# Attention scores of a hybrid encoder layer: 128-row matmuls over stacked high and low parts instead of pairs of 64-row matmuls, and a reordered prologue of three weight tiles

## The reference, cut to what matters

```
proj = h @ w_in[l]
qa, ka, va, qb, kb, vb, ga, gb = jnp.split(proj, pts, axis=-1)
...
# diff_attention: 8 heads, two 64-wide maps m = 0, 1 of each, chunk-causal, 128-query blocks
s = jnp.einsum('bqhmd,bkhmd->bhmqk', qb, k).astype(jnp.float32) * scale + bias[None, :, None]
s = jnp.where(mask, s, NEG_INF)
p = jax.nn.softmax(s, axis=-1)
attn = p[:, :, 0] - lam * p[:, :, 1]
return jnp.einsum('bhqk,bkhe->bqhe', attn, vf)
```

## Time and profile before

| | |
|---|---|
| median of the runs | 1826.25 us (3 runs, lowest 1825.3, highest 3576.29) |
| the profiled execution, its own time | 1823.93 us |
| its span from the first to the last instruction | 1822.1 us |
| granted TensorE clock, mean | 0.998 |
| busy share: PE, DVE, ACT, POOL | 98%, 58%, 39%, 36% |

### The profile page before, as it was taken

The page is one execution under the profiler, slowest core; times in us unless marked ns, Lnnn a source line. Parts: engine busy times, 40 slices in busy tenths (PEclk is TensorE's granted clock), DMA queues, the critical chain, the costliest instruction groups (busy, mean ns, idle before and its releaser), DMA issues.

```text
span 1822.1 us, 25660 instructions
## 1 busy us (share of the span) xinstructions
PE 1783.3 (98%) x9007; PEld 1453.0 (80%) x9007; DVE 1048.4 (58%) x2291; ACT 701.6 (39%) x1544; POOL 661.9 (36%) x662
## 2 busy tenths in 40 slices
PE   5999999999999999999999999999999999999998
PEld 4777777777778888888888878788888888888886
DVE  5366666656665554111432565677766666777767
ACT  5355555555556666310222132322223333222232
POOL 4311112111123444322222250465555656655560
PEclk9999999999999999999999999999999999999999
DMA  6411111111111101134322440121121111111112
GB/s 239 140 35 33 49 36 36 47 34 35 44 34 43 33 24 36 46 81 160 103 83 91 140 153 0 59 69 46 46 69 46 46 46 46 56 59 46 60 45 92
DMA packets 143398, 117.91 MB, mean 65 GB/s; under 512 B 23556, under 2 KB 130252, under 8 KB 143308
## 3 DMA queue, kind: packets, MB, share of 16 engines
q1 hardware_dynamic: 134092, 112.52, 20.1%
q10 hardware_dynamic: 9216, 4.20, 0.8%
HBM read 99.88 MB, written 21.53 MB: 67 GB/s over the span
## 4 chain that ended last, share of the span: by engine, by line
PE 88%; DVE 4%; ACT 3%; POOL 3%; issue 2%; DMA 0%; SPq 0%; ACTq 0%; DVEq 0%; POOLq 0%
PE bank L569 27%; PE bank L571 26%; PE bank L570 26%; PE bank L607 4%; PE bank L595 3%; PE bank L655 2%; POOL w_lo L1190 1%; ACT mix L971 1%; DVE mix L1476 1%; DVE mix L1455 1%; POOL hT_lo L1207 1%; PE bank L656 1%; DVE y_lo L1329 0%; ACT w_hi L862 0%; ACT mix L1025 0%
## 5 line engine op out<-in xcount | busy, mean ns | idle before, releaser
L569 PE MATMUL bank<-hT_hi,w_hi 128*128 128x512 f32 x1312 | 528.0, 402 | 9.0 <-POOL hT_lo L1207 5.9
L571 PE MATMUL bank<-hT_hi,w_lo 128*128 128x512 f32 x1312 | 512.3, 390 | 0.0
L570 PE MATMUL bank<-hT_lo,w_hi 128*128 128x512 f32 x1312 | 512.3, 390 | 0.0
L1190 POOL TENSOR_TENSOR w_lo<-w_raw,w_hi 128x256 fp32r<-128x256 f32 x264 | 189.3, 748 | 616.9 <-ACT w_hi L862 616.9
L569 PEld LDWEIGHTS bank<-hT_hi,w_hi 128*128 128x128 f32 x1312 | 246.5, 188 | 82.7 <-issue 16.7
L571 PEld LDWEIGHTS bank<-hT_hi,w_lo 128*128 128x128 f32 x1312 | 246.7, 188 | 53.6
L570 PEld LDWEIGHTS bank<-hT_lo,w_hi 128*128 128x128 f32 x1312 | 247.1, 188 | 46.2
L569 PE MATMUL bank<-y_hi 128*128 128x512 f32 (+1 forms) x548 | 205.9, 376 | 0.8 <-issue 0.8
L570 PE MATMUL bank<-y_lo,y_hi 128*128 128x512 f32 (+1 forms) x548 | 203.3, 371 | 0.0
L571 PE MATMUL bank<-y_hi,y_lo 128*128 128x512 f32 (+1 forms) x548 | 203.2, 371 | 0.0
L1271 POOL TENSOR_TENSOR y_lo<-y_full,y_hi 128x512 fp32r<-128x512 f32 x98 | 131.8, 1377 | 165.6 <-ACT y_hi L1125 165.6
(11 more groups left out here) (172 smaller groups left out, 2856.9 us busy)
## 6 DMA issues: line engine op xcount, KB each, us to landing
w_raw<-in_w_in_dram SPq DMA_DIRECT2D x100, 256.0 KB, 3.3
w_raw<-in_w_ff_dram SPq DMA_DIRECT2D x64, 256.0 KB, 4.1
y_full<-in_w_ff_dram SPq DMA_DIRECT2D x32, 512.0 KB, 3.7
bias_rows<-bias_line SPq DMA_DIRECT2D x3, 1536.0 KB
res<-in_x_dram SPq DMA_DIRECT2D x8, 512.0 KB, 6.3
x_spill<-res SPq DMA_DIRECT2D x8, 512.0 KB, 5.9
o_spill<-o_buf ACTq DMA_DIRECT2D x64, 64.0 KB, 1.6
w_raw<-in_w_branch_b_dram SPq DMA_DIRECT2D x16, 256.0 KB, 3.9
```

The lines of the kernel that those rows point to most:

```text
L569: pe.matmul(bank, lhs[0], rhs[0], start=start, stop=False)
L570: pe.matmul(bank, lhs[0], rhs[1], start=False, stop=False)
L571: return pe.matmul(bank, lhs[1], rhs[0], start=False, stop=stop)
L1190: ins = pool.tensor_tensor(w[1][:, n % 2, at:at + 2], w_raw[:, at:at + 2, :], w[0][:, n % 2, at:at + 2].bitcast(F32), ALU.subtract)
```

## The change

Q and k of the first attention are laid out anew. For each map m the moving operand `k_a[slot][m]` is one 128-row tensor: the high part of k of this map on its own 64 partitions, and the low part on the other 64. The stationary operand is `q_a[slot][m]`: part 0 holds the high part of q on both halves, part 1 the low part on the map's own half and zeros on the other. So a block of scores is 4 matmuls of 128 rows in place of 6 matmuls of 64 rows, and each map waits for its bank by itself. Filling these tensors takes 4 ACT copies of 64 partitions for a half group of `qa` (before, 1 of 128), 2 for `ka` (before, 1), and 2 DVE operations for each (before, 1). POOL zeroes the empty halves once for each slot. The second attention keeps its 64-row matmuls.

The prologue has a third weight buffer (`w_third`, in a part of `y_lo` that is not yet used), and runs the half groups by token halves: tiles 0, 1, 2 for the first 512 tokens, then tiles 0, 1, 2 for the others. `w_lo` of tiles 1 and 2 is now DVE's. One pass of row statistics (row tile 7) moves behind the first eight token tiles, the load of weight tile 0 behind four rows of x, and its split on ACT behind three normalised rows.

```diff
-ORDER = [(0, 0), (1, 0), (0, 1), (1, 1)]
+FIRST = 3
+ORDER = [(_n, _half) for _half in range(2) for _n in range(FIRST)]
 for _n, (_kind, _i) in enumerate(TILES):
-    if _n < 2:
+    if _n < FIRST:
...
+        ROWS = (slice(0, HD), slice(HD, P))
+        q_odd = [nc.alloc_sbuf_tensor_at(f"q_odd{i}", [P, 2, SEQ], F32R, offset=y_at + (4 * KT + 2 + 2 * i) * SEQ * 4) for i in range(2)]
+        q_a = [[[t[:, m, :] for t in pair] for m in range(2)] for pair in (y, q_odd)]
+        k_a = [[t[:, 2 + slot, :] for t in y] for slot in range(2)]
+        w_third = [y[1][:, 4 + part, :].rearrange("p (t c) -> p t c", t=KT) for part in range(2)]
...
+            return w_third[part] if n == FIRST - 1 else w[part][:, n % 2]
...
-            for n in range(2 * KT):
-                half, kt = n // KT, n % KT
+            for n in range(KT):
                 pe.wait_ge(h_lo, n + 1)
-                group(0, half, [kt])
-                if kt < 4:
+                group(0, 0, [n])
+                if n < 4:
                     turn_tokens(n + 4)
-                if kt == KT - 1:
-                    group(1, half, range(3))
-                    if half == 0:
-                        for m in range(KT, KT + 4):
-                            turn_tokens(m)
-                    group(1, half, range(3, KT))
-            for half in range(2):
-                group(2, half)
+            group(1, 0)
+            for n in (KT, KT + 1):
+                turn_tokens(n)
+            for kt in range(0, KT, 2):
+                group(2, 0, range(kt, kt + 2))
+                turn_tokens(KT + 2 + kt // 2)
+            for kt in range(KT):
+                pe.wait_ge(h_lo, KT + kt + 1)
+                group(0, 1, [kt])
+                if kt < 2:
+                    turn_tokens(KT + 6 + kt)
+            for n in (1, 2):
+                group(n, 1)
...
-                        scores([SCORE[("a", h, i, m, c)] for m in range(2)], h % 2,
-                               [([t[:, h % 2, i * P:(i + 1) * P] for t in q], slice(c * HALF, min((c + 1) * HALF, (i + 1) * P)), 0)])
+                        keys = slice(c * HALF, min((c + 1) * HALF, (i + 1) * P))
+                        for m in range(2):
+                            unit = SCORE[("a", h, i, m, c)]
+                            if unit >= 3:
+                                pe.wait_ge(scores_read, unit - 2)
+                            for part in range(2):
+                                mm = pe.matmul(SC[unit % 3][:, 0:keys.stop - keys.start], q_a[h % 2][m][part][:, i * P:(i + 1) * P],
+                                               k_a[h % 2][m][:, keys], start=part == 0, stop=part == 1)
+                            mm.then_inc(scores_done, 1)
...
-                    if n >= 2:
-                        act.wait_ge(gemm_done, LAST[n - 2] + 1)
-                    act.activation(w[0][:, n % 2], w_raw[:, :, :], ACT.Copy).then_inc(w_hi_done, 1)
+                    if n >= FIRST:
+                        act.wait_ge(gemm_done, LAST[n - 2 if n != FIRST + 1 else 0] + 1)
+                    act.activation(w_tile(n, 0), w_raw[:, :, :], ACT.Copy).then_inc(w_hi_done, 1)
...
-                    act.activation(q[0][:, h % 2, cols], src, ACT.Copy, scale=SCALE).then_inc(qk_hi, 1)
+                    for m in range(2):
+                        for rows in ROWS:
+                            ins = act.activation(q_a[h % 2][m][0][rows, cols], src[ROWS[m]], ACT.Copy, scale=SCALE)
+                    ins.then_inc(qk_hi, 1)
+                elif kind == "ka":
+                    for m in range(2):
+                        ins = act.activation(k_a[h % 2][m][ROWS[m], cols], src[ROWS[m]], ACT.Copy)
+                    ins.then_inc(qk_hi, 1)
...
                     normed(t - 1)
-                else:
-                    split_weights(0)
+            split_weights(0)
             normed(3)
             deviation(4)
             for n in range(KT):
                 tokens_hi(n)
-                if n % 2 and n < KT - 1:
-                    deviation(5 + n // 2)
-                    normed(4 + n // 2)
+                if n in (1, 4):
+                    deviation(5 + n // 4)
+                    normed(4 + n // 4)
                 if n == 3:
                     act.wait_ge(line_done, 1)
                     act.activation(line_sb, SC[0][0:A_HEADS + B_HEADS, 0:LINE], ACT.Copy).then_inc(line_sb_done, 1)
-                if n == 4:
+                if n == 5:
                     split_weights(1)
+            deviation(NT - 1)
+            normed(NT - 2)
+            group_hi(0, 0)
             normed(NT - 1)
-            group_hi(0, 0)
+            split_weights(2)
             for n in range(KT, 2 * KT):
                 tokens_hi(n)
-                if n == KT + 2:
-                    group_hi(1, 0)
+                if n in (KT + 1, KT + 6):
+                    group_hi(1 + (n - KT) // 6, 0)
             act.wait_ge(lam_dve, 1)
             act.activation(lam_e[:, 2:4], lam_e[:, 0:2], ACT.Exp).then_inc(lam_act, 1)
             group_hi(0, 1)
-            split_weights(2)
             group_hi(1, 1)
-            split_weights(3)
-            for half in range(2):
-                group_hi(2, half)
+            split_weights(FIRST)
+            group_hi(2, 1)
...
+            def zero_rows(pair):
+                for m in range(2):
+                    pool.memset(pair[m][1].bitcast(F32), 0.0).then_inc(q_zero, 1)
+
+            zero_rows(q_a[0])
...
-            splits[0] = 2
-            for n in range(2, TILE[("qb", 1)] + 1):
+            splits[0] = FIRST
+            bias_a_rest(0)
+            pool.wait_ge(spilled, 16 * NT)
+            zero_rows(q_a[1])
+            for n in range(FIRST, TILE[("qb", 1)] + 1):
                 split_weights(n)
                 kind, i = TILES[n]
-                if kind == "qa" and i >= 1 or n == 2:
+                if kind == "qa":
...
+                elif kind == "qa":
+                    dve.wait_ge(q_zero, 2 * (h % 2 + 1))
+                    pieces = [[t[ROWS[m], cols] for t in q_a[h % 2][m]] + [bank[ROWS[m], :]] for m in range(2)]
                 else:
-                    hi, lo = (t[:, h % 2, cols] for t in (q if kind == "qa" else k))
-                dve.scalar_tensor_tensor(lo, GEMM[g % 2][:, :], 1.0 if kind in ("ka", "kb") else SCALE, hi.bitcast(F32), ALU.mult, ALU.subtract).then_inc(freed_dve, 1)
+                    pieces = [[k_a[h % 2][m][rows, cols] for rows in (ROWS[m], ROWS[1 - m])] + [bank[ROWS[m], :]] for m in range(2)]
+                for hi, lo, src in pieces:
+                    ins = dve.scalar_tensor_tensor(lo, src, 1.0 if kind in ("ka", "kb") else SCALE, hi.bitcast(F32), ALU.mult, ALU.subtract)
+                ins.then_inc(freed_dve, 1)
...
+            def weights_lo(n):
+                dve.wait_ge(w_hi_done, n + 1)
+                dve.tensor_tensor(w_tile(n, 1), w_raw[:, :, :], w_tile(n, 0).bitcast(F32), ALU.subtract).then_inc(w_lo_done, 1)
+
             for n in range(KT):
                 tokens_full(n)
-                if n % 2 and n < KT - 1:
-                    moments_in(5 + n // 2)
-                    scales(4 + n // 2)
+                if n in (1, 4):
+                    moments_in(5 + n // 4)
+                    scales(4 + n // 4)
+                if n == 6:
+                    weights_lo(1)
+            moments_in(NT - 1)
+            scales(NT - 2)
             scales(NT - 1)
-            dve.wait_ge(w_hi_done, 2)
-            dve.tensor_tensor(w[1][:, 1], w_raw[:, :, :], w[0][:, 1].bitcast(F32), ALU.subtract).then_inc(w_lo_done, 1)
             qk_lo(0, 0)
+            weights_lo(2)
             for n in range(KT, 2 * KT):
                 tokens_full(n)
-                if n == KT + 2:
+                if n == KT + 1:```

The order of ACT in the second head, from the exponential of step 1 to that of step 2. Ahead of it PE ends a half group of the next `qa`. Before (L879 is the copy of the half group, L868 the splits, L960 and L963 `out_rows`):

```order
L971 ACTIVATE mix,small<-mix,small 128x256 x2
L879 ACTIVATE y_hi<-bank 128x512
L868 ACTIVATE y_lo<-bank 128x128
L960 ACTIVATE o_buf<-o_buf,small 128x128
L963 ACTIVATE unused,small<-o_buf,small 128x128
L952 DMA o_spill<-o_buf 128x128
L868 ACTIVATE y_hi<-bank 128x4x128 x2
L862 ACTIVATE w_hi<-w_raw 128x1024
L971 ACTIVATE mix,small<-mix,small 128x384 x2
```

28 lines of the change are left out of this document (17 added, 11 removed).

## The result

The changed kernel takes **1864.6 us**, the one before 1825.8 in the same session: a ratio of 1.0213, with an interval of 1.0199 to 1.0227. That is 38.8 us slower, where I had forecast about 20, and 3.6 above my range. The profiled execution took 1865.2 us, its span is 1863.2. Each of the two kernels also had one execution in a slow state (2969.2 and 3576.3 us), which no comparison here uses.

What follows compares the result with a forecast made beforehand. It took PE, busy 98% of the span, as the bound. On the profiled 1823.9 us, -20.2 - 6.4 + 35.1 + 4.0 + 2.1 + 5 = +19.6 gave 1843.5, say 1844 us, range 1830 to 1860.

Steps and rivals of the forecast that it cites:

- Score blocks, -20.2: First attention's heads on PE: 96 blocks each save 0.21 us, 20.2 us less; bounds 96 x 0.15 and 96 x 0.25.
- rival A: In the heads, the copies stay hidden because the chain has unseen slack, PE stays the bound; 1803 us, chance 0.13.
- Rival C: Score blocks on PE: four full matmuls cost what the old block cost, nothing saved there; 1852 us, chance 0.10.
- The start, -6.4: Prologue: the new order brings the first scores at about 63.5 instead of 69.92, 6.4 us sooner; bounds 0 and -8.
- The copies, +35.1: Heads: extra ACT and DVE operations make PE wait at step 1's values and step 4's second map, 35.1 us in sum.
- Small waits, +6.1: Heads: PE arrives sooner and waits longer, 4.0 us for `w_lo` and 2.1 us for `combine` at head openings.
- The clock, +5: Behind PE's wait at step 4 the clock falls, costing 1.0 us in five heads, +5; bounds 0 and +12.
- Rival D: Heads: two slow-clock stretches follow each hole at step 4, making the kernel over 2% slower; 1863 us, chance 0.07.

Runs made afterwards that it cites:

- e3: Changed kernel with one 128x512 copy and one subtraction per half group, so scores sum over wrong rows; 1807.1 us, ratio 0.9897 to the kernel before.
- e1: Changed kernel with the start of the kernel before, heads keeping the stacked scores and all copies; 1867.3 us, ratio 1.0226 to the kernel before.
- e4: Changed kernel, all copies kept, probabilities ahead of the query half group at step 1, VectorE's half groups of steps 2 and 3 behind the next row maxima; 1822.5 us.
- e7: Changed kernel with matmuls by a tile of zeros filling TensorE's two holes in each head; 1861.9 us, ratio 1.0202 to the kernel before.
- e2: Kernel before, its 64-row scores kept, with only the copies out of the banks made like the changed kernel's; 1880.3 us, ratio 1.0302.
- e9: Changed kernel with transfers inside SBUF replacing two of ScalarE's four copies per query half group, except in the first head; 1842.1 us, ratio 1.0097 to the kernel before.

## Why the prediction was right and wrong, step by step

**Score blocks, -20.2: right.** 1.36 us and equal steps at 512 keys. The smaller blocks save a little less than I gave them: at 128 keys e3 has 0.79 us where I had 0.73, since a dense matmul behind 128-column ones still comes 0.28 us ahead of the next (68.72 and 69.00 in the changed kernel); so the wide steps do not stand only beside 64-row matmuls. Over the heads of e3, 56.4 us against 58.2 with 0.3 more of waiting for `w_lo`, the blocks give some 2.1 a head, 17 in all, inside my bounds. e3 as a whole is rival A's case, forecast at 1803, measured at 1807.1. Rival C is refuted by both. Where the Trainium skill, "TensorEngine Tiling (Array Packing)" (Performance Considerations), packs contractions of at most 64 rows, the stacked form took less here, 1.36 us against 1.54. Whether the wide steps of the packed form were the drain that I took them for, no run shows.

**The start, -6.4: the size was wrong.** The first scores came at 68.33 in place of 63.5 and so moved by 1.6. Three things were missing. The last triple of the first half group began at 33.19, not 1 us ahead of the 32.11 before but 1.1 behind it: 2.1. Behind it the clock was low for one stretch from 33.6, as it was in the earlier trace rows before, and I had counted every matmul at 0.227: about 1.7. And I priced the copies only inside the heads, while they stand in the start too; that is the last 1 us or so. e3, without the second copies, comes at 67.11, only 2.8 ahead of the kernel before. The 5.8 of e1 looks like my 6.4 only because the old order pays more for the copies, which the kernel before does not make.

**The copies, +35.1: the mechanism and both places right, the size wrong, and this is the step that failed.** I wrote that each further copy costs 0.47 and the second subtraction 0.61, the steps of two 128-row operations in a row. Those steps hold an overlap, and operations that change from one half of the partitions to the other have none: 2.62 and 1.42 in place of 2.0 and 1.1. Twice 2.62 and 1.42 are 6.7 us a head, where I had 5.1; at full clock the waits come to 4.8 (23.1 - 18.3) + 1.9 = 6.7. That the waits on the page sum to only 5.2 or so in most heads (1.9 and 3.3), just my number, is chance: in four of the six heads TensorE comes to step 4 later, at the low clock, and waits less; in the two with a full clock on the way the wait is 4.8. Six heads give 40. In the first head I guessed 2.0 + 1.9; the wait at the values was 3.7 where e3 has 1.1, and from there to step 4 it took 102.7 - 79.1 = 23.6 where e3 takes 93.4 - 75.3 = 18.1: 2.6 + 5.5 = 8.1 in place of 3.9. Together 48 in place of 35. That the last head pays nothing was right (57.6 us from its values to the next ones), and so it seems that the copies of `ka` at step 5 are hidden: TensorE has no wait for ScalarE or VectorE between them and the opening of the next head.

**Small waits, +6.1.** Mostly right where TensorE sets the pace: in e3 the waits for `w_lo` are 6.0, against 3.0 before, and in e4 they are 7.8. In the changed kernel they vanish into the other holes.

**The clock, +5: right in place and about right in size.** Behind step 4, where I had put it, the low stretches cost 5 to 6 us in all (e7). I had not foreseen those behind the values, and they cost nothing, since the chain sets that stretch. Rival D named nearly the right total, 1863, for the wrong reason: two low stretches follow the hole in two heads of six, and the clock cost about a quarter of the 7 x 3.4 = 24 that D gave it.

**The sum, with what was measured.** e3 against before is -18.2; the copies at the start add 1.2, since e3's first scores come at 67.11; the chain +48. To the +38.8 measured 7.8 are then left, of which 5 to 6 are the clock and the rest stays open. Against the forecast's +19.6 the chain is 13 of the 19 that were missing, the start and the other terms of TensorE 3.5, the clock and the open rest 2.8.

For VectorE's share of what was missing, 0.2 of the 0.6 us, a rule stands in the Trainium skill, "VectorE: DVE Perf Modes" (Two Vector instructions with no wait between them): an instruction is held until the earlier ones have finished when its operands start in another group of partitions than the last one's. The DVE rows above agree: from 164.24 to 164.94 and 165.66 the steps are 0.70 and 0.72 us for operations of 0.68 and 0.69, where the earlier trace rows have 0.61 behind one of 0.69. ScalarE's share, 0.4, is shown by its own rows in e2.

## What to carry to other kernels

Work that is taken off the busiest engine and handed to two idle ones is free only if it does not stand between their hand-overs: add up the chain from one wait of the busy engine to the next, and compare it with that engine's own time for the same stretch. Where the chain is the longer one, ask first what it does not need there; putting the copies behind what the next hand-over needed gave 42 us in two moves, 21 of them for the row maxima alone, while filling the holes to hold the clock gave nothing clear of noise. Price a split operation by the step of operations of just that kind, in the order of partitions in which they will stand.

## What the runs showed of the hardware that I had not expected

- ScalarE overlaps two copies in a row by 0.09 us (step 0.50, length 0.59) when they read and write the same half of the partitions, and not at all when the half changes (step 0.59). A change of the destination alone is enough: in the changed kernel the two copies of one map read the same half of the bank and write the two halves, and its four copies start 0.60 apart throughout (2.41 us in all). Whether a change of the source alone would do it too, no run shows; in e2 both change together.
- The transfers inside SBUF that ScalarE issues in e9 took no visible time of its own work. Two issues (ACTq) lie beside its copies, which stand 0.59 apart, as without them:

```profile
215.14 0.47 ACTq L986 DMA_DIRECT2D q_odd<-q_odd  x1
...
215.40 0.57 ACT L911 ACTIVATE y_hi<-bank 64x512 fp32r<-64x512 f32 x1
215.65 0.61 ACTq L986 DMA_DIRECT2D q_odd<-q_odd  x1
215.99 0.59 ACT L911 ACTIVATE y_lo<-bank 64x512 fp32r<-64x512 f32 x1
```

- The clock fell behind small holes too. In e4, which has no wait over 1.1 us in these heads, two stretches ran low, each right behind a wait of 1.0 us for `w_lo` (at 219.53 and 397.04):

```profile
219.60:223.00 3.40, 3.40 (x8) 2.70 (x9) 1.86 (x4) 1.98 (x7) 0.00 (x0) 0.51 0.60 174
279.90:283.30 3.40, 3.40 (x15) 2.83 (x16) 1.88 (x4) 2.01 (x7) 0.00 (x0) 1.00 0.60 173
397.10:400.50 3.40, 3.40 (x8) 2.68 (x9) 1.87 (x4) 1.99 (x7) 0.00 (x0) 0.50 0.60 171
```

The same wait of 1.0 us in the head behind the first, at 279.85, had no such effect, nor had it in four other heads. What tells the two cases apart is open.
